# One value product per chunk instead of two in the gated recurrence: the masked scores of both directions are added on VectorE

## The reference

```python
def hgrn2_chunked(q, k, v, logf):          # chunks of 64 tokens
    ...
    qe = q * jnp.exp(bcs - ref)
    ke = k * jnp.exp(ref - bcs)
    A = jnp.where(mask, jnp.einsum('bcthk,bcshk->bchts', qe, ke), 0.0)
    o_intra = jnp.einsum('bchts,bcshv->bcthv', A, v)
    ...
    o_inter = jnp.einsum('bcthk,bchkv->bcthv', q * jnp.exp(bcs), prev)
    return (o_intra + o_inter).reshape(b, T, H, V)

o_fwd = hgrn2_chunked(qp, kp[:, :, 0], vp, lfp[:, :, 0])
o_bwd = _flip(hgrn2_chunked(_flip(qp), _flip(kp[:, :, 1]), _flip(vp), _flip(lfp[:, :, 1])))
o = (o_fwd + o_bwd)[:, npad:]
```

## Time and profile before

| | before |
|---|---|
| median of 3 runs | 2535.94 us (2533.18 to 2542.76) |
| the profiled execution | 2537.11 us, span 2535.6 us |
| TensorE matmul busy | 2378.0 us (94%) |
| TensorE weight loads busy | 2042.9 us (81%) |
| VectorE busy | 897.4 us (35%) |
| ScalarE busy | 831.0 us (33%) |
| GpSimd busy | 787.2 us (31%) |
| mean granted TensorE clock | 0.977 of full speed |

### The profile page before, as it was taken

One profiled execution on the slowest core, in us unless ns is written; L12 is line 12 of the kernel. 1 busy time (PEld: TensorE's weight loads), 2 busy tenths in 40 slices (PEclk: granted clock), 3 DMA queues, 4 the chain that ended last, 5 costly groups with the idle time before them and its releaser, 6 DMA issues.

```text
span 2535.6 us, 35934 instructions
## 1 busy us (share of the span) xinstructions
PE 2378.0 (94%) x13672; PEld 2042.9 (81%) x13672; DVE 897.4 (35%) x1300; ACT 831.0 (33%) x972; POOL 787.2 (31%) x434
## 2 busy tenths in 40 slices
PE   4999999998879889999999999998998999999996
PEld 3888888887767767788888888877886888888885
DVE  5101101013867878642555555543223111011113
ACT  3331111122224324241555555543213331121222
POOL 2232223223334323333433333322333222233221
PEclk9999999999889999999999999999998999999999
DMA  2222122213101101113211111112231222212121
GB/s 77 66 64 60 58 63 62 63 57 104 42 26 34 33 25 41 33 51 108 67 42 42 38 38 41 42 34 59 78 120 47 61 58 66 64 56 70 58 60 64
DMA packets 251286, 144.22 MB, mean 57 GB/s; under 512 B 4752, under 2 KB 247616, under 8 KB 251216
## 3 DMA queue, kind: packets, MB, share of 16 engines
q1 hardware_dynamic: 248880, 130.73, 18.3%
q0 software_dynamic: 2336, 12.58, 1.4%
HBM read 133.86 MB, written 9.44 MB: 57 GB/s over the span
## 4 chain that ended last, share of the span: by engine, by line
PE 71%; issue 12%; DVE 10%; POOL 3%; ACT 2%; DMA 1%; SPq 0%; DVEq 0%; POOLq 0%; ACTq 0%
PE slot L406 62%; DVE ca L1218 2%; POOL wlo L1544 2%; PE aux L542 1%; PE aux L651 1%; PE aux L528 1%; POOL q L1664 1%; PE aux L512 1%; PE aux L538 1%; DVE e L1300 1%; DVE sq L1074 1%; PE aux L619 1%; PE aux L644 1%; PE aux L632 1%; PE aux L480 0%
## 5 line engine op out<-in xcount | busy, mean ns | idle before, releaser
L1544 POOL TENSOR_TENSOR wlo<-raw,whi 128x1024 fp32r<-128x1024 f32 x218 | 539.8, 2476 | 1337.9 <-ACT whi L725 1337.9
L406 PE MATMUL slot<-xh,whi 128*128 128x512 f32 (+2 forms) x2704 | 720.3, 348 | 50.4 <-ACT xh L742 29.5
L406 PE MATMUL slot<-xh,wlo 128*128 128x512 f32 (+2 forms) x2704 | 706.1, 343 | 0.0
L406 PE MATMUL slot<-xl,whi 128*128 128x512 f32 (+2 forms) x2704 | 698.6, 341 | 0.0
L406 PEld LDWEIGHTS slot<-xh,whi 128*128 128x128 f32 x2704 | 510.0, 191 | 128.6 <-issue 35.8
L406 PEld LDWEIGHTS slot<-xh,wlo 128*128 128x128 f32 x2704 | 515.2, 191 | 60.8
L406 PEld LDWEIGHTS slot<-xl,whi 128*128 128x128 f32 x2704 | 511.9, 190 | 59.4
L725 ACT ACTIVATE whi<-raw 128x1024 fp32r<-128x1024 f32 x241 | 253.6, 1052 | 301.6 <-PE slot L406 289.3
L1097 DVE TENSOR_TENSOR prod<-gate,slot 128x784 f32<-128x784 f32 (+1 forms) x44 | 42.4, 963 | 617.5 <-PE slot L406 617.5
L406 PE MATMUL slot<-ah,whi 128*128 128x272 f32 (+1 forms) x704 | 181.7, 340 | 0.0
L406 PE MATMUL slot<-ah,wlo 128*128 128x272 f32 (+1 forms) x704 | 181.7, 340 | 0.0
(11 more groups left out here) (252 smaller groups left out, 2492.4 us busy)
## 6 DMA issues: line engine op xcount, KB each, us to landing
raw<-in_ffn_w_gate_up SPq DMA_DIRECT2D x88, 512.0 KB, 3.8
raw<-in_w_in SPq DMA_DIRECT2D x81, 512.0 KB, 3.9
raw<-in_ffn_w_down SPq DMA_DIRECT2D x32, 448.0 KB, 3.6
raw<-in_ffn_w_down SPq DMA_DIRECT2D x16, 512.0 KB, 3.8
raw<-in_ssd_w_proj SPq DMA_DIRECT2D x8, 512.0 KB, 3.8
raw<-in_hg_w_proj SPq DMA_DIRECT2D x8, 512.0 KB, 3.7
raw<-in_w_out SPq DMA_DIRECT2D x8, 512.0 KB, 3.9
h_spill<-h POOLq DMA_DIRECT2D x1, 3072.0 KB, 9.8
```

Source lines behind the costliest of these rows:

```text
L406: mm = pe.matmul(slot[b][:, PC + u:PC + v], w[b][:, t, :], x[:, t, u + off:v + off], start=(t == 0 and p == 0 and q == 0), stop=(t == k - ...
L1544: pool.tensor_tensor(wlo[s % 2][:, :, :], raw[s % 2][:, :, :], whi[s % 2][:, :, :].bitcast(F32), ALU.subtract).then_inc(w_lo, 1)
```

## The change

A new pair of buffers `both[s]` (128x128, float32) is allocated, and a new semaphore `as_ok`. After the two predicated copies of a chunk, VectorE waits for the second one (`am_ok`) and adds the two buffers into `both[p % 2]`. TensorE waits for `as_ok` and makes one value product with it where it made two. What the scores' own PSUM reuse waits for (`am_ok`) is unchanged.

```diff
@@ memory of the recurrence
-            am=[[new(f"am{s}{d}", [P, P]) for d in range(2)] for s in range(2)]))
+            am=[[new(f"am{s}{d}", [P, P]) for d in range(2)] for s in range(2)], both=[new(f"both{s}", [P, P]) for s in range(2)]))
@@ TensorE, hg_outputs
                     if p + 1 < NC:
                         within(p + 1)
-                    pe.wait_ge(am_ok, lin(12 * j + 2 * p + 2, 24, i))
+                    pe.wait_ge(as_ok, lin(6 * j + p + 1, 12, i))
                     out = aux2[1][:, 2 * P + P * p:2 * P + P * (p + 1)]
-                    for d in range(2):
-                        pe.matmul(out, m_h["vt"][:, p, :], m_h["am"][p % 2][d][:, :], start=(d == 0), stop=False,
-                                  skip_group_check=True)
+                    pe.matmul(out, m_h["vt"][:, p, :], m_h["both"][p % 2][:, :], start=True, stop=False, skip_group_check=True)
@@ VectorE, hg_masks
                     for d in range(2):
                         dve.copy_predicated(m_h["am"][p % 2][d][:, :], incl64[d][:, :].bitcast(I32),
                                             aux[1 - p % 2][:, P * d:P * (d + 1)]).then_inc(am_ok, 1)
+                    w(am_ok, 12 * j + 2 * p + 2, 12)
+                    dve.tensor_tensor(m_h["both"][p % 2][:, :], m_h["am"][p % 2][0][:, :], m_h["am"][p % 2][1][:, :], ALU.add).then_inc(as_ok, 1)
```

More of the change, by code:

```diff
@@ L252, in build @@
         f_ok, ln_ok, bc_ok, d_ok, e_ok, k_ok, q_ok = (sem(n) for n in ("f_ok", "ln_ok", "bc_ok", "d_ok", "e_ok", "k_ok", "q_ok"))
-        ht_mm, ht_ok, kv_mm, kv_ok, a_mm, am_ok, o_mm = (
-            sem(n) for n in ("ht_mm", "ht_ok", "kv_mm", "kv_ok", "a_mm", "am_ok", "o_mm"))
+        ht_mm, ht_ok, kv_mm, kv_ok, a_mm, am_ok, as_ok, o_mm = (
+            sem(n) for n in ("ht_mm", "ht_ok", "kv_mm", "kv_ok", "a_mm", "am_ok", "as_ok", "o_mm"))
         osq_ok, os_mm, ors_ln, ors_ok, yb_ok = (sem(n) for n in ("osq_ok", "os_mm", "ors_ln", "ors_ok", "yb_ok"))
```

## The result

The changed kernel took 2551.21 us, the median of 20 runs (2528.17 to 2559.73), against 2536.26 us for the kernel before (20 runs, 2531.20 to 2542.76). The ratio is 1.0041 with a 95% interval of 1.0021 to 1.0060: slower, where 0.28% faster was forecast, and the median lies 14 us above the forecast range. (The ratio of the medians is 1.0059; that of the means is 1.0040, as the faster runs pull at it.) The scatter says more than the median. Before, all runs lie within 12 us.

What follows compares the result with a forecast made beforehand. It took TensorE's alternation of weight loads and matmuls as the bound at the outputs. 10.9 us removed, less holds, left 7.1 us gained: 2528.8 us from a median of 2535.94, 0.28% less, with a range of 2523 to 2537 us.

Steps and rivals of the forecast that it cites:

- The sum: Over eight heads: products removed save 10.9 us, TensorE's holds for the addition taken off, leaving 7.1 us gained.
- Removed loads: TensorE's value products in 6 chunks of 8 heads: 192 weight loads become 96, 0.2225 us saved per chunk.
- addition: VectorE's added 128x128 float32 sum in each chunk, 48 in all, taken as 0.284 us each.
- its wait: VectorE's wait for the result of the masked copy ahead of each addition, taken as 0.06 us.
- holds in chunk 0: TensorE's value product in chunk 0 of each head held 0.33 us for the addition.
- chunk 5: TensorE's value product in the last chunk of each head held 0.14 us for the addition.
- the estimate of 194 ns: VectorE's addition by the skill page's table, 58 + 128 cycles at 0.96 GHz; would give about 8.5 us gain, 2527.4 us.
- The gain passes down: After the outputs, ScalarE and all that follows start earlier; TensorE's 1.69 us low-part wait stays; full 7.1 us kept.
- the new holds bring TensorE's clock down: Rival: half clock in seven heads' outputs, 1.25 us a head, 8.8 us in all, 2537.6 us; chance 0.05.
- hidden: Rival: VectorE's additions hidden altogether, holds about zero, gain 9.5 to 10.9 us, about 2525.5 us; chance 0.12.
- dear: Rival: VectorE's addition takes 0.64 us plus a 0.11 us wait, +2.2 us in all, about 2538 us; chance 0.05.
- the gain taken up later: Rival: TensorE's later 1.69 us wait grows by what was won, gain 0 to 1 us, 2535.5 us; chance 0.10.

Runs made afterwards that it cites:

- fill_before: The kernel before, with two overwritten TensorE products ahead of the last state product and two ahead of chunk 1's scores; 2535.3 us, 0.9989 of before.
- fill_gaps: The changed kernel with two overwritten TensorE products ahead of the last state product and two ahead of chunk 1's scores; 2527.4 us, 0.9963 of before.
- after_again: The changed kernel unaltered, run once more beside other experiments; 2553.4 us, 1.0045 of the kernel before.
- hold_only: The changed kernel, but TensorE makes both value products per chunk after waiting for the addition, whose result is unused; 2542.0 us, 1.0013 of before.
- one_direction: The kernel before with one value product per chunk, from the first direction's masked scores alone, and no addition; 2533.8 us, 0.9984 of before.
- late_idle: The changed kernel with one overwritten product in each of chunks 3, 4 and 5, after the wait for the sum; 2542.2 us, 1.0022 of before.
- second profile: Profile of one execution of the unaltered changed kernel, from the run after_again; that execution took 2556.49 us.
- filler: The changed kernel with one overwritten product in chunk 0 of each head, ahead of the wait for the addition; 2529.3 us, 0.9963 of before.
- hold_double: hold_only with a second addition in chunk 0, so TensorE is held about twice as long; 2543.8 us, 1.0027 of before.

## Why the prediction was wrong

**The sum was right.** Removed loads, addition (292 ns against 284), its wait (0.04 us against 0.06), holds in chunk 0 (0.27 us against 0.33) and chunk 5 (0.13 against 0.14), none between, and a head's outputs shorter by 0.89 us against 0.865. For the addition the row of 284 ns was the better guide; the estimate of 194 ns beside it was a third too low. The gain passes down as argued: the wait for the low weight part kept its length. That the execution without a fall in the first seven heads took 2527.89 us, near the 2528.8 of the forecast, is in part luck. The forecast for an execution like the profiled one was 2530.0, and of the 9.2 us between 2537.11 and 2527.89 some 1.5 were won ahead of the first head's value product (1271.78 in place of 1273.29 us), which the change doesn't touch. The sum itself rests on the 7.1 us between `fill_before` and `fill_gaps`.

**The step that failed is the rival "the new holds bring TensorE's clock down".** I gave it 0.05, against it "0.33 more is little", and priced it at 1.25 us a head; the sum has no term for the clock at all. In its place the runs showed a loss of 15.0 us (16.2 in `after_again`) where 7.1 were to be won, and idle work in TensorE's waits gave 26 us back. Three things were wrong. The price: a long fall costs 8.0 us in a head, since it lasts through the rest of the outputs, 17 us at half clock, not over chunk 0 alone. I took the length from the one fall in the last head of before, which ended after 3.4 us with two value products in each chunk, and such products were just what the change removes. The cause: the hold by itself cost 1.5 us beyond the sum (`hold_only`), the missing products by themselves 6.2 (`one_direction`), both together 23. And my list of what is removed counted the products only as time saved; with three of them put back as idle work the falls are shorter (`late_idle`).

**The range** came from rivals that were each priced from one profile. With a long fall in three of seven heads and 4.1 us more in the last, as in the second profile, the forecast would have been 2528.8 + 3 x 8.0 + 4.1 = 2556.9 us; the median was 2551.2. No row of before could have given these prices.

**The rivals on the addition** (hidden, dear) and the gain taken up later were all wrong, as forecast.

In the chance of "within 0.5%" the ratio of 1.0041 is still inside; the direction was not.

The section "HAM oscillation — how this bites in real kernels" of the page "TensorE: Matmul & The Clock Gate" in the Trainium skill says that idle gaps throttle the array. The 26 us of `fill_gaps` agree with that in kind, but the page's case has DMA waits of microseconds, and here no single wait is over 0.77 us. The section tells only of gaps. That the clock stayed at half for 16 us with TensorE shown as busy in every one of them is not explained by it.

**Open.** Which head has a fall in an execution differs from one to the next, and what decides it no run shows. That the thin mix of loads and short matmuls keeps the clock down is the reading that fits `late_idle` and `one_direction`; it is not shown. What the hold does is open too: without it the falls in the thinned kernels were about as many, but shorter, and `filler` had a long one with its hold filled. Each kernel but the changed one and `late_idle` has one profile, too few to say more than that the longest fall was 10.2 us in `late_idle` and 17.1 in the changed kernel.

## What to carry to other kernels

Before products are taken off TensorE next to waits, look at the granted clock of that stretch, and ask what the clock would be with less work in it; here a saving of 7 us ended as a loss of 16. If runs of one kernel split into groups, take several profiles and compare the waits head by head. Idle products in waits that exist anyway cost nothing here (ScalarE's wait is 12.15 us with them and 12.14 without, where the clock is full), and they were worth more than the saving itself.

## What I had not expected of the hardware

- TensorE's clock stayed at 0.50 for 17 us while its busy time was 16.92 of 17 us in the window, and came back only about 2 us into the dense projection.
- A hold of 0.6 us behind waits of 1.7 us cost no clock with 14 to 16 loads a chunk (`hold_double`, 6.3 us for 4.9 us of holds); with 12 to 14 loads a hold of 0.27 us went with a loss of 23 us beyond the sum.
- Falls at half clock in the changed kernel's outputs all began within 0.5 us of the same instruction, the load of chunk 0's value product, in 8 of 28 heads, and lasted 3.4, 6.8 or 17.1 us.
- Four idle products a head, in waits that exist, were worth 26 us in the changed kernel and 2.1 in the kernel before.
